# A transformer stack on one core: the norm's root read out of PSUM, half of a norm's sums ahead of the last output unit, constant products in six places

## What is computed

```python
def rms_norm(x, g):
    return x * rsqrt(mean(x * x, axis=-1) + EPS) * g

def first_block(x, mem, ...):
    xa, zu, zv, ga, gb = split(rms_norm(x, g) @ w_in)
    ya = s5_branch(xa)           # state-space scan, gelu; y * sigmoid(y @ w_glu)
    yb = sgu_branch(zu, zv)      # gelu, layer norm, spatial gate
    h = x + (sigmoid(ga) * (ya @ w_proj_a) + sigmoid(gb) * (yb @ w_proj_b)) @ w_out
    h = h + memory_cross_attention(rms_norm(h, g), memn)      # w_q ... w_o
    h = h + swiglu(rms_norm(h, g))
    return rms_norm(h, g)

def second_block(x, ctx, ...):                    # two layers, l = 0, 1
    for l in range(2):
        hx, hc = modulate(rms_norm(x)), modulate(rms_norm(ctx))
        x = x + g_m * mixer(hx, keys and values of hx and hc)
        if l == 0:
            ctx = ctx + g_m * mixer(hc)
            ctx = ctx + g_f * swiglu(modulate(rms_norm(ctx)))
        x = x + g_f * swiglu(modulate(rms_norm(x)))
    return rms_norm(x)
```

## Time and profile before

| | |
|---|---|
| three runs | 2359.42, 2355.76, 2358.92 us; median 2358.92 us |
| profiled execution | 2358.22 us, span 2356.4 us |
| mean granted TensorE clock | 0.971 |
| DMA queues of the core | 393 MB, 167 GB/s over the span |

### The profile page before, as it was taken

How to read it: one execution, slowest core, us unless ns; L and a number is a source line. 1 busy time by engine, 2 the same in 40 slices (tenths; PEclk the granted TensorE clock), 3 DMA queues, 4 the chain that set the end, 5 groups by cost and what they waited for, 6 DMA issues and landing times.

```text
span 2356.4 us, 41646 instructions
## 1 busy us (share of the span) xinstructions
PE 2192.0 (93%) x17181; PEld 2048.3 (87%) x17181; DVE 1618.6 (69%) x2081; ACT 1005.8 (43%) x1189; POOL 206.9 (9%) x201
## 2 busy tenths in 40 slices
PE   8898998999999889999999779999999977999998
PEld 6675996899999878999999668999999976889998
DVE  8887564655588776655578968665467896866554
ACT  4113445543444554433444355444344435544432
POOL 3762003000000110000000110000000011100000
PEclk9999999999999999999999899999999988999999
DMA  7678774565554433455555222455545532234651
GB/s 247 237 282 311 246 271 154 166 197 194 176 168 155 126 108 126 162 186 188 188 175 165 90 72 91 158 164 187 198 152 176 154 108 72 90 126 145 194 196 72
DMA packets 290483, 393.09 MB, mean 167 GB/s; under 512 B 8518, under 2 KB 256668, under 8 KB 283676
## 3 DMA queue, kind: packets, MB, share of 16 engines
q1 hardware_dynamic: 285620, 383.53, 49.6%
q10 hardware_dynamic: 3624, 6.31, 0.8%
q0 software_dynamic: 1088, 1.10, 0.2%
HBM read 387.66 MB, written 3.15 MB: 166 GB/s over the span
## 4 chain that ended last, share of the span: by engine, by line
PE 76%; DVE 14%; ACT 4%; issue 3%; DMA 2%; POOL 1%; DVEq 0%; SPq 0%; ACTq 0%
PE L L849 60%; PE M L849 3%; DVE w_rest L432 3%; PE L L1100 2%; PE M L983 2%; PE L L1086 2%; ACT w_high L426 1%; PE M L1336 1%; DVE work L2601 1%; PE L L1113 1%; DVE work L2473 1%; DMA raw<-in_w_ada 1%; DVE m L1967 1%; PE L L1169 1%; DVE n_rest L1976 1%
## 5 line engine op out<-in xcount | busy, mean ns | idle before, releaser
L849 PE MATMUL L<-n_high,w_high 128*128 128x256 f32 x3360 | 955.8, 284 | 19.9 <-DVE w_rest L432 7.1
L849 PE MATMUL L<-n_rest,w_high 128*128 128x256 f32 x3360 | 939.8, 280 | 0.0
L849 PE MATMUL L<-n_high,w_rest 128*128 128x256 f32 x3360 | 939.7, 280 | 0.0
L432 DVE TENSOR_TENSOR w_rest<-raw,w_high 128x2048 fp32r<-128x2048 f32 x293 | 671.2, 2292 | 231.6 <-PE L L849 225.1
L426 ACT ACTIVATE w_high<-raw 128x2048 fp32r<-128x2048 f32 x293 | 561.1, 1915 | 380.1 <-PE L L849 341.6
L849 PEld LDWEIGHTS L<-n_high,w_high 128*128 128x128 f32 x3360 | 639.9, 190 | 40.9 <-issue 30.7
L849 PEld LDWEIGHTS L<-n_rest,w_high 128*128 128x128 f32 x3360 | 638.4, 190 | 0.6
L849 PEld LDWEIGHTS L<-n_high,w_rest 128*128 128x128 f32 x3360 | 638.0, 190 | 0.0
L849 PE MATMUL L<-hid_high,w_high 128*128 128x256 f32 x768 | 214.8, 280 | 3.1 <-DVEq L2396 3.1
L849 PE MATMUL L<-hid_high,w_rest 128*128 128x256 f32 x768 | 213.8, 278 | 0.0
L849 PE MATMUL L<-hid_rest,w_high 128*128 128x256 f32 x704 | 196.0, 278 | 0.0
(11 more groups left out here) (396 smaller groups left out, 2800.4 us busy)
## 6 DMA issues: line engine op xcount, KB each, us to landing
raw<-in_w_in SPq DMA_DIRECT2D x116, 1024.0 KB, 5.5
raw<-in_w_ffn SPq DMA_DIRECT2D x99, 1024.0 KB, 5.3
raw<-in_w_ada SPq DMA_DIRECT2D x32, 1024.0 KB, 6.4
raw<-in_w_out SPq DMA_DIRECT2D x16, 1024.0 KB, 5.3
raw<-in_w_gate SPq DMA_DIRECT2D x11, 1024.0 KB, 5.3
raw<-in_w_up SPq DMA_DIRECT2D x11, 1024.0 KB, 5.4
raw<-in_w_down SPq DMA_DIRECT2D x11, 1024.0 KB, 5.0
work<-in_w_ada SPq DMA_DIRECT2D x8, 1024.0 KB, 7.4
```

The lines of the kernel that those rows point to most:

```text
L432: nc.vector.tensor_tensor(w_rest[:, u.first % 2, :], raw[:, u.first % 4, :], w_high[:, u.first % 4, :].bitcast(F32), ALU.subtract).then_in ...
L849: ins = mm(dst, a, b, start=first and i == 0, stop=last and i == 2, skip_group_check=skip)
```

## The change

It has five parts.
1. For norms 2 to 12 the root reads the sums in `M[:, 0]`: the activation scales by 1/D and adds EPS as its bias, a new third word of `flat`, set once by GpSimd at the start. It waits for the sums (`sum_ready`) and for the scalings of all earlier norms (`scaled`), since it overwrites `rstd`. VectorE's `mean_of` is gone, and its readers wait for the root (`root_ready`).
2. For norms 2, 3, 6, 8 and 11 the sums of chunks 0 to 3 go in front of the last unit (unit 3) of the output projection, chunks 4 to 7 behind it. ScalarE's squares of the first three banks move between the units of that projection (`linear_squared`).
3. The constants behind those sums go from 6 to 4 (norm 2) and from 10 to 8 (the others).
4. In front of `glu` TensorE multiplies 5 constants; in x0 and x1 it multiplies 6 in front of the swap of `qk` and 18 behind `proj0`.
5. In c0 it multiplies 2 in front of each of `gate0`'s units 2 and 3 and 2 behind `proj0`, in c1 2 behind `dv`.

```diff
--- before.py
+++ after.py
@@ -227,7 +227,7 @@
-        flat = sb("flat", [P, 2])
+        flat = sb("flat", [P, 3])
@@ -761,13 +761,14 @@
             nc.gpsimd.memset(flat[:, 1:2], 1.0).then_inc(flats_set, 1)
+            nc.gpsimd.memset(flat[:, 2:3], EPS).then_inc(flats_set, 1)
...
-            pool.wait_ge(flats_set, 3)
+            pool.wait_ge(flats_set, 4)
@@ -971,17 +972,22 @@
-            def keep_busy(n):
+            def keep_busy(n, bank=1):
 
                 for _ in range(n):
-                    mm(M[:, 1, 0:T], ones[:, :], dft64[:, :], start=True, stop=True)
-
-            def norm(k, spare=0):
-
-                for c in range(DC):
+                    mm(M[:, bank, 0:T], ones[:, :], dft64[:, :], start=True, stop=True)
+
+            def norm_sums(k, c0, c1):
+
+                for c in range(c0, c1):
                     pe.wait_ge(sq_ready, 4 * k + c // 2 + 1)
-                    ins = mm(M[:, 0, 0:T], ones[:, :], m[:, c, :], start=c == 0, stop=c == DC - 1)
-                ins.then_inc(sum_ready, 1)
+                    ins = mm(M[:, 0, 0:T], ones[:, :], m[:, c, :], start=c == 0, stop=c == DC - 1, skip_group_check=True)
+                if c1 == DC:
+                    ins.then_inc(sum_ready, 1)
+
+            def norm(k, spare=0, c0=0):
+
+                norm_sums(k, c0, DC)
                 keep_busy(spare)
@@ -1243,6 +1249,7 @@
             name = "glu"
+            keep_busy(5)
             pe.wait_ge(branch_ready, 1)
@@ -1268,8 +1275,14 @@
-            cols_linear("out", before=mid_hooks("out"), chunk=split_chunk(1))
-            norm(2, 6)
+            out_hooks = mid_hooks("out")
+
+            def before_last():
+                if 3 in out_hooks:
+                    out_hooks[3]()
+                norm_sums(2, 0, 4)
+            cols_linear("out", before={**out_hooks, 3: before_last}, chunk=split_chunk(1))
+            norm(2, 4, 4)
@@ -1290,14 +1303,15 @@
-            cols_linear("mem_o", before={1: lambda: turn_modulation(0, 2), 2: lambda: pe.wait_ge(ada_row, ADA_GROUPS)}, chunk=split_chunk(2))
+            cols_linear("mem_o", before={1: lambda: turn_modulation(0, 2), 2: lambda: pe.wait_ge(ada_row, ADA_GROUPS),
+                                         3: lambda: norm_sums(3, 0, 4)}, chunk=split_chunk(2))
...
-                norm(k, 10)
+                norm(k, 8, 4)
@@ -1319,7 +1333,7 @@
-                    pe.wait_ge(ms_ready, NORM_OF[p] + (2 if p == "c0" else 1))
+                    pe.wait_ge(root_ready, NORM_OF[p] + (2 if p == "c0" else 1))
@@ -1377,6 +1391,8 @@
                 def swap_qk():
+                    pe.wait_ge(d_rot, 3 * rx + 1)
+                    keep_busy(6, 0)
                     pe.wait_ge(qk_n, num + 1)
                     pe.wait_ge(d_rot, 3 * rx + 2)
@@ -1402,6 +1418,7 @@
                     rows_linear(p + "dv", before={1: square_sums})
+                    keep_busy(2)
                     continue
@@ -1434,10 +1451,16 @@
                     whole_units(p + "proj0", 0, before={0: swap_qk})
+                    keep_busy(18, 3)
                     pe.wait_ge(d_rot, 3 * rx + 3)
                 else:
-                    cols_linear(p + "gate0")
+
+                    def stay_busy():
+                        pe.wait_ge(qk_ms, num + 1)
+                        keep_busy(2)
+                    cols_linear(p + "gate0", before={2: stay_busy, 3: stay_busy})
                     whole_units(p + "proj0", 0)
+                    keep_busy(2)
@@ -1453,14 +1476,14 @@
-                cols_linear(p + "out", chunk=split_chunk(3 + nf))
+                cols_linear(p + "out", before={3: lambda: norm_sums(FFN_NORM[p], 0, 4)}, chunk=split_chunk(3 + nf))
...
-                pe.wait_ge(ms_ready, 13)
+                pe.wait_ge(root_ready, 13)
@@ -1491,19 +1514,24 @@
-            def squares_of(k, h):
+            def squares_of(k, h, b0=0, b1=4):
...
-                for b in range(4):
+                for b in range(b0, b1):
                     if k in BEFORE_NORM:
                         act.wait_ge(bank_free[b], after(BEFORE_NORM[k], b))
...
             def root_of(k):
-                act.wait_ge(ms_ready, k + 1)
-                A(rstd[:, :], rstd[:, :], ACT.Sqrt).then_inc(root_ready, 1)
+                if k < 2:
+                    act.wait_ge(ms_ready, k + 1)
+                    A(rstd[:, :], rstd[:, :], ACT.Sqrt).then_inc(root_ready, 1)
+                else:
+                    act.wait_ge(sum_ready, k + 1)
+                    act.wait_ge(scaled, SCALED[k])
+                    A(rstd[:, :], M[:, 0, 0:T], ACT.Sqrt, scale=1.0 / D, bias=flat[:, 2:3]).then_inc(root_ready, 1)
@@ -1512,8 +1540,12 @@
-            def norm(k, h, shift, split=True):
-                squares_of(k, h)
+            def linear_squared(name, k, h):
+
+                linear(name, None, {b + 1: (lambda b=b: squares_of(k, h, b, b + 1)) for b in range(3)})
+
+            def norm(k, h, shift, split=True, b0=3):
+                squares_of(k, h, b0)
                 root_of(k)
@@ -1735,7 +1767,7 @@
-            linear("out", None)
+            linear_squared("out", 2, hx)
...
-            linear("mem_o", None)
+            linear_squared("mem_o", 3, hx)
...
-                linear(p + "out", None)
+                linear_squared(p + "out", FFN_NORM[p], h)
                 feed_forward(p, h, lambda c: mod[:, l, s * 48 + 24 + c:s * 48 + 25 + c])
-            norm(12, hx, None, split=False)
+            norm(12, hx, None, split=False, b0=0)
@@ -1955,10 +1987,6 @@
-            def mean_of(k):
-                dve.wait_ge(sum_ready, k + 1)
-                V.tensor_scalar(rstd[:, :], M[:, 0, 0:T], 1.0 / D, EPS, ALU.mult, ALU.add).then_inc(ms_ready, 1)
-
@@ -1981,7 +2009,6 @@
             def norm(k, h, gain, shift, split=True, dst=None):
-                mean_of(k)
                 inverse_root(k)
@@ -2427,7 +2454,7 @@
-                    linear(name, beside={6: lambda: mean_of(next_), 7: lambda: (inverse_root(next_), scale_chunks(src, g_, 0, 4)),
+                    linear(name, beside={7: lambda: (inverse_root(next_), scale_chunks(src, g_, 0, 4)),
@@ -2481,7 +2508,7 @@
-                    linear(p + "dk", beside={0: lambda: mean_of(10), 1: lambda: (v_out(), inverse_root(10))})
+                    linear(p + "dk", beside={1: lambda: (v_out(), inverse_root(10))})
@@ -2555,7 +2582,7 @@
-                    linear(p + "conv_u", beside={1: lambda: (modulation_out(1, 1), mean_of(5))})
+                    linear(p + "conv_u", beside={1: lambda: modulation_out(1, 1)})
```

## The result

The changed kernel is slower: median 2368.35 us over 20 runs against 2358.11 us over 20 runs of the kernel before (means 2366.9 and 2358.1). The ratio on record is 1.0034 with a 95% interval of 1.0018 to 1.0051, which is +8 us, between +4 and +12. A second set of six runs gave 1.0072 (1.0044 to 1.0100). The forecast was +3 us and "no change that can be told, leaning slow". Its lean was right and its size too small: by the forecast's own line of 0.2% the change is slower, which it gave 0.25. The median is 0.9 us above its range for 8 in 10 (2352.5 to 2367.5); the ratio on its base of 2358.92 gives 2366.9, just inside.

What follows compares the result with a forecast made beforehand. TensorE, busy 93% of the span, was taken as the bound in most stretches, VectorE in others. Terms +3.65 - 0.46 + 1.58 - 1.3 - 0.4 - 0.1 = +2.97 us: 2358.22 to 2361.2; 8-in-10 range 2352.5 to 2367.5.

Steps and rivals of the forecast that it cites:

- Root out of PSUM: Last norm: scaling and hand-over leave the path, -0.46 us; nothing in norms where TensorE has other work.
- Sums ahead of the last unit: Norms 2, 3, 6, 8, 11: 1.79 us of sums moved forward, root 0.73 us later each, +3.65 us together.
- B (hidden sums): Five norms: TensorE waits before the last unit, so the moved sums cost nothing, 1.06 us back each; 2352.2 us, 5%.
- C (load behind the waits): Roots with two waits: table loaded after the wait for sums, +6.2 us, 2367.4 us; 13%.
- D: Roots: the skill page's drain of about 1380 ns comes with each table switch; 2369 us, 1%.
- Glu: Five constants before glu's unit follow the idle wait: 2.24 us added, 0.66 taken up later, +1.58 us.
- the same stretch at half speed passes whatever runs in it: At glu: TensorE's lower-clock stretch stays equally long, so the five constants add their full 2.24 us.
- c0 and c1: Constants partly fill TensorE's waits: 0 in c0; -0.1 us in c1, where the next unit waits for w_rest anyway.
- VectorE as the bound to the end of proj0: In c0: w_rest goes without a wait, so filling TensorE's wait before gate0's third unit gains 0.
- x0 and x1: Constants before qk's swap and after proj0 fill waits, so attention runs less at low clock: -1.3 and -0.4 us.
- the 1.51 us: x0's attention: VectorE takes its second pair of maxima 1.51 us late, the possible gain; -1.3 was taken.
- Rival A: Filled waits in attentions, swaps, c0, c1: all time lost at low clock returns, -11.6 us, 2351.4 us; 15%.

Runs made afterwards that it cites:

- the one whose wait was filled: Kernel before with only the root out of PSUM, plus 8 constants ahead of TensorE's wait for ScalarE's last early output at glu; ratio 0.9984, mean 2355.9 us.
- the third kernel: Changed kernel with the sums of all five norms put back behind the last unit, all new constants kept; ratio 1.0013 to the kernel before, mean 2364.8 us.
- the narrow products: 32-column constant products, 17 per ffn_up, added to four kernels; ratios to kernel before: before 1.0052, changed 1.0104, root only 1.0051, root and constants 1.0063.

## Why the prediction was right or wrong

**Root out of PSUM: right.** Forecast -0.46 in the last norm: -0.37 to -0.57 in twelve profiles. Where it stands alone it gives 0.30 to 0.50 at each of the other five.

**Sums ahead of the last unit: right.** Forecast +0.73 each: the six profiles with them have +0.62 to +0.80 at the five norms, mean 0.74. The table load ends last now, as said. Rivals B (hidden sums), C (load behind the waits) and D fell with the rows of norm 3: the load stands directly ahead of the root, and TensorE ran the moved sums and the last unit without a gap. What I left unsaid is that with the root out of PSUM alone the norm costs 0.40 less than before, so the sums ahead cost 1.14 each of what the change could have had, 5.7 us.

**Glu: right where the lower level stayed, and it did not always stay.** Forecast +1.58. Five of seven profiles with these constants have +1.51 to +1.55; the two of the unaltered changed kernel have -0.14, with no low stretch at the unit. The step "the same stretch at half speed passes whatever runs in it" failed in those: the low stretch was not there. Of the seven profiles without these five constants it is missing only in the one whose wait was filled, so the constants may have shifted it off; two cases don't show it. The mean is +1.06.

**c0 and c1: wrong.** Forecast 0 and -0.1. c1 costs +1.45 in the profiles (2.00 against 0.55). The step that failed is the sentence that the unit behind the wait may be 1.7 us faster while the next waits for w_rest. Both halves are right, and the conclusion left out what that second, longer wait does to the clock. c0 is not settled: -1.45 with and -1.98 without its constants in the mean, each with a spread of 3 us and more. The reason given for 0, VectorE as the bound to the end of proj0, was not tested.

**x0 and x1: wrong.** Forecast -1.3 and -0.4; measured +0.3 and +0.5, which cannot be told from nothing. In the first profile the mechanism seems to work at the start of x0's attention. VectorE's rows in the changed kernel, where the pair of maxima that waited 1.51 us in the earlier trace rows waits 0.35, and a later row of the same attention:

```profile
1337.74 1.29 DVE L2108 TENSOR_REDUCE soft<-M 128x1 f32<-128x512 f32 x2 [0.35 <-PE M L1018]
...
1401.19 0.69 DVE L2129 TENSOR_TENSOR work_r<-L,work_r 128x512 fp32r<-128x512 f32 x1 [2.99 <-ACT work_r L1601]
```

Against the rows of before the first is 1.17 us nearer to the swap (1337.44 before, with the changed kernel 1.47 us late at the swap). The second stood at 1398.11 with a wait of 1.37, so by then 2.8 us had been lost. In the changed kernel TensorE was at its lower level there, in the kernel before it was not (windows, changed and then before):

```profile
1390.50:1401.00 10.50, 7.50 (x46) 6.83 (x44) 6.02 (x10) 5.57 (x11) 0.00 (x0) 0.84 0.32 100
```

```profile
1389.00:1398.00 9.00, 5.97 (x47) 5.42 (x45) 6.05 (x10) 5.65 (x12) 0.00 (x0) 1.00 0.39 118
```

But the wait of that pair in the other profiles shows that even the early gain was luck. Here it is in the third kernel (all constants), and in the kernel before with the narrow products (none of them):

```profile
1345.33 1.29 DVE L2101 TENSOR_REDUCE soft<-M 128x1 f32<-128x512 f32 x2 [1.68 <-PE M L1018]
```

```profile
1335.36 1.29 DVE L2083 TENSOR_REDUCE soft<-M 128x1 f32<-128x512 f32 x2 [0.26 <-PE M L1014]
```

With the 6 and 18 constants the pair waits 0.35, 0.34, 1.16, 1.37, 1.68 and 1.78 us, without them 0.26, 0.33, 0.47, 1.11, 1.17, 1.51, 1.69 and 1.70. The wait goes with the end of the last low stretch ahead of it, counted from the same weight subtraction at the swap: an end at 35.8 to 36.5 us goes with waits of 0.26 to 0.47, one at 37.4 with 1.11 to 1.17, one at 37.9 to 38.8 with 1.37 to 1.78, with or without constants. The constants delayed the start of that stretch (at 30.6 to 33.1 us with them, 23.8 to 27.2 without) and left its end in the same range. So the step that failed is the one that took the 1.51 us as what the constants win back. The attentions behind have low stretches in every profile, and where they fall differs from run to run. I read the price of their places from one trace and took it as fixed. The Trainium skill, "TensorE: Matmul & The Clock Gate", HAM oscillation, counts half of the throttled time as lost; here the changed kernel has less of it (clock 0.979 against 0.971) and is slower. As c1's two units show, throttled time counts where the others wait for TensorE (+2.00) and not where TensorE would wait anyway. Rival A fell with that.

**The sum.** With the measured terms: 5 x 0.74 - 0.48 + 1.06 + 1.45 + 0.3 + 0.5 + 0.5 (c0, unsettled) = +7.0 us, against +2.97 forecast and +4 to +12 measured. The term that was mis-sized is the constants: forecast -0.2, measured about +3.8 in the ledger, of which 2.5 (glu and c1) stand clear in the profiles and 1.3 (x0, x1, c0) do not. The times of the kernels, in us with standard errors, put more on the sums than the ledger does, and less on the constants:

| step | ledger | times |
|---|---|---|
| root alone | -2.5 | -1.0 (1.8), with narrow products +0.7 (1.6) |
| sums ahead, no constants | +5.7 | +9.1 (2.6) |
| sums ahead, with constants | +5.7 | +4.4 (2.3), with narrow products +8.5 (2.3) |
| constants, no sums ahead | +3.8 | +5.5 (2.3), with narrow products +2.4 (1.5) |
| constants, with sums ahead | +3.8 | +0.8 (2.6) |

That the forecast's range nearly held the result is in part luck: the gains that it took for x0 and x1 did not come, c1's cost was left out, and the range was wide enough to hold +8 us.

**The pace.** It was in none of my terms. The scatter that I took from three runs, 3.7 us, is really 20 us, and it sets what one profile can tell: over the ten profiles without the narrow products, the time goes with the number of slow matmuls (correlation 0.94; 3666 slow distances at 2352.52 us, 8665 at 2377.11).

**Open.** The means lie above what their ledgers give on top of 2359.2, at standard errors of 1.2 to 2.1 us: by 6 us for the sums without constants (2368.4 against 2362.5), by 3 for the changed kernel (2369.2 over all 26 runs against 2366.2), by 4 for root with constants, by 3, 2 and 0 for root alone and the changed kernel without c1's and without x0's and x1's constants. The memory attention does not explain it: against the trace of before it has +1.4 us in the mean with sums ahead and +1.8 without. That sums ahead make a slow ffn_up more likely could explain a part, but the profiles do not show it: 9 of 20 slow with them, 6 of 20 without. One narrow product for each group of four units, instead of three, would cost some 5 us in all (a third of the 15 us in the ledger), against 6.7 us for the 1.5 slow ffn_ups of a mean run, and might keep all of them fast; it was not tried.

## What to carry to other kernels

Work moved ahead of the last unit of a saturated engine buys latency with throughput: price the norm by what ends last after the move, and try the cheap part (here the root straight out of PSUM) alone first. Constants that fill a wait make the engine early for its next wait, and a low-clock stretch then falls on other work. None of the six places here showed a gain, so look first at what the work behind the filled wait waits for, and whether it has slack of its own. Before a term of 1 us is read from one profile of a kernel whose runs lie 20 us apart, find what the runs differ by, and read each term from stretches cut at the same instructions in several profiles of both kernels.

## What the runs showed that was not expected

TensorE's stream of 128x256 matmuls with a weight load each runs at 113 or at 118 ns, at the same granted clock of 1.00. The pace holds for over 1,000 matmuls (4.5 us an ffn_up), changes almost only where the stream is interrupted, and differs from run to run of one kernel. Why there are two is open. A float32 product with 32 columns in front of units set it to 113 ns in 16 of 16 ffn_ups. Behind the constants with 256 columns both paces were seen.
